# A mixture-of-experts stage with other load shapes, another gather and another order of its matmuls

## The chip, the cores and the metric

The kernel runs on one core of one Trainium2 chip. The metric is the device time of one execution in microseconds (us). The three runs of the kernel before took 984.13, 984.41 and 986.63 us, so the median is 984.41 us. The profile was taken of one execution by the hardware profiler.

A core has five engines with instruction streams of their own: TensorE (PE, whose weight loads are listed as PEld), VectorE (DVE), ScalarE (ACT), GpSimd (POOL) and SyncE (SP), which here issues the DMAs. They meet through semaphores. The matrix memory SBUF has 128 partitions; matmuls write to eight banks of PSUM, 512 fp32 words wide.

## The reference

One decoder layer on 512 tokens of width 1024. The part that matters here is the second of its three blocks, a mixture of 32 experts of which every token uses two:

```python
u = rms_norm(h, norm_ffn_g[l])
# every token: the best of 4 groups, in it the best 2 of 8 experts, with gates from two softmaxes
# every expert e, for the rows that chose it (fp32):
h_e = silu(x_e @ w_gate_e[e]) * (x_e @ w_up_e[e])     # (rows, 1024) @ (1024, 512), twice
y_e = h_e @ w_down_e[e]                               # (rows, 512) @ (512, 1024)
h = h + sum over the two choices of gate * y
```

Ahead of it stands a recurrent and pooling block (dense projections, about the first 370 us of the profile), behind it a gated per-layer embedding (`h + sigmoid(u @ w_ple_gate) * (p @ w_ple)`) and a last RMSNorm. The weights of the experts are 32 x 3 x 2 MB = 201 MB.

## The kernel before

Tokens are held as four tiles of 128 rows (`TT` = 4), the width as eight k-tiles of 128 (`KD`), an expert's hidden width of 512 as four (`KF`). `ring` is a ring of eight slots of 2 MB in SBUF; the three matrices of an expert (gate, up, down) each fill one slot. The SP stream loads matrix m + 8 into the slot of matrix m once PE has read that one (`wait_expert_read`), so at most eight matrices are loaded or in use, and SP's loads go out in the order in which PE reads them.

An expert takes up to `C` = 64 rows in one round. The number of rounds is read from a register (`rounds_i`); for these inputs one round runs. Inside it a loop runs four times over a body of eight experts (`UNROLL`), so PE, DVE, ACT, POOL and SP all branch back three times. For each expert:

- DVE makes `pick`, a 0/1 matrix [token, row] per token tile, by comparing `iota` with `place` (L975), and copies that expert's `info` (row number and gate) to `pinfo` (L1027).
- PE gathers the rows: `pick` is the stationary operand (64 columns), the normed tokens `u2` the moving one, in fp32, two halves of the width into the upper and lower 64 partitions of bank 0. ACT copies them to `xrow` (L731), PE transposes them (L1261), ACT copies the result to `xT` (L735). With `gather_info` PE also brings row number and gate into row order, and DVE's `take_info` copies them out (L1030, L1031).
- PE multiplies `xT` with gate and up (L1117, 128x256 moving, 32 matmuls; each fp32 matmul appears twice in the trace), again in two halves of partitions of bank 2.
- ACT takes the sigmoid (L746), DVE multiplies twice (L1048, L1050), PE transposes the hidden rows (L1294), DVE copies them to `hT` (L1052).
- PE multiplies `hT` with down (128x512 moving), DVE scales by the gate (L1058), and POOL scatters the 64 rows to `expert_rows` in HBM (L558). Four buffers `yrow` are in turn; `row_free` says that a scatter has landed.

On PE the order within an expert is: gate and up of e, gather for e + 1, transposes of hidden(e), info of e + 1, transposes of the rows of e + 1, down of e. Every line that goes through the helper `mm` shows as L1117, so in the trace the tiles and shapes tell the matmuls apart.

After the last expert SP waits for the last scatter and loads `expert_rows` back in eight pieces (L465); DVE adds them to the residual `h1` (L1070); POOL and DVE make the low parts of `w_ple_gate` (L339) from the high parts that ACT rounded (L755). Two-part operands exist there and in the dense blocks: a value is rounded to fp32r (`high`) and the rest kept as fp32r too (`low`); an fp32r matmul appears once in the trace.

## Time and profile before

| what | us |
|---|---|
| runs, lowest / median / highest | 984.13 / 984.41 / 986.63 |
| span of the profiled execution, first to last instruction (no time apart from its span is given for it) | 986.3 |
| first gate matmul of expert 0 to the end of the down product of expert 31 | 395.45 to 905.4 |
| PE busy over the span | 923.1 (94%) |
| DVE / ACT / POOL busy | 369.2 / 259.6 / 129.0 |
| bytes moved by DMA | 255.12 MB, of these 248.46 MB on SP's queue |
| mean granted TensorE clock | 0.967 of full |

A span's rows can be read on four levels. The page gives shares of the whole span; the timeline gives single instructions (start, duration, engine, line, operation, tiles, shapes, count; in brackets the idle time before and what ended it); windows give busy time and the granted clock of a stretch; the DMA view gives bytes and packets of each queue. TensorE's ends are modelled, so what one matmul costs in a row of matmuls is read from the distance between starts. The page says that the chain of waits that ended last is 78% PE, 13% DVE, and that DMA is busy for nine tenths and more in every slice from about 415 us to 890 us.

### The profile page before, as it was taken

How to read it: one execution, taken by the hardware profiler on the slowest of the kernel's cores; microseconds unless marked ns; L12 is line 12 of the kernel's file. 1: busy time of each engine (PE TensorE's matmuls, PEld its weight loads, DVE VectorE, ACT ScalarE, POOL GpSimd, SP SyncE). 2: the span in 40 equal slices, each digit the busy share in tenths (PEclk: the TensorE clock that was granted, in tenths of full speed). 3: DMA queues.
4: the chain of work that ended last, by engine and by line, in shares of the span. 5: the costliest groups of instructions: out<-in, count | busy, mean ns of one | idle time of the engine just before them, and what ended most of it. 6: DMA issues, size and time to landing. Idle time of an engine off the chain costs nothing.

```text
span 986.3 us, 13206 instructions
## 1 busy us (share of the span) xinstructions
PE 923.1 (94%) x5579; PEld 586.0 (59%) x5579; DVE 369.2 (37%) x580; ACT 259.6 (26%) x359; POOL 129.0 (13%) x85
## 2 busy tenths in 40 slices
PE   4999995999999996999998999989999899999796
PEld 3678773888888873545544554545455445554485
DVE  5699898464243424111111111111211121111764
ACT  6464445352132132111010101010101110112347
POOL 3328942000000000000000000000000000001320
PEclk8899997999999997999999999999999899999799
DMA  9122221122144749799999999999999999992702
GB/s 260 57 86 85 86 86 43 67 105 86 67 147 171 276 174 359 252 398 394 396 393 396 394 397 394 396 394 392 394 395 394 391 391 394 395 396 84 274 1 86
DMA packets 112898, 255.12 MB, mean 259 GB/s; under 512 B 8562, under 2 KB 9654, under 8 KB 112840
## 3 DMA queue, kind: packets, MB, share of 16 engines
q1 hardware_dynamic: 109848, 248.46, 67.7%
q0 software_dynamic: 2560, 4.20, 1.2%
q10 hardware_dynamic: 432, 1.57, 0.4%
q8 instruction: 49, 0.80, 0.3%
q14 instruction: 9, 0.07, 0.0%
HBM read 247.93 MB, written 10.49 MB: 262 GB/s over the span
## 4 chain that ended last, share of the span: by engine, by line
PE 78%; DVE 13%; ACT 3%; issue 2%; SPq 2%; DMA 2%; DVEq 0%; POOLq 0%; ACTq 0%
PE bank L1117 74%; DVE ring L873 2%; DVE ring L877 2%; PE bank L1261 2%; PE bank L1294 1%; DVE ring L885 1%; DVE ring L859 1%; DVE r L879 1%; DMA ring<-in_w_in_dram 1%; DVE r L1070 1%; PE bank L1131 1%; DVE ring L878 1%; SPq L395 1%; ACT ring_rounded L324 1%; DVE ring L875 1%
## 5 line engine op out<-in xcount | busy, mean ns | idle before, releaser
L1117 PE MATMUL bank<-ring_rounded,ring_rounded 128*128 128x512 f32 x704 | 248.0, 396 | 1.7 <-ACT ring L760 1.7
L1117 PE MATMUL bank<-ring,junk 128*64 128x256 f32 x2048 | 232.7, 386 | 9.7 <-issue 8.9
L1117 PE MATMUL bank<-r_rounded,ring_rounded 128*128 128x512 f32 x704 | 232.9, 402 | 1.4 <-DVE ring_rounded L817 1.3
L1117 PEld LDWEIGHTS bank<-ring,junk 128*64 128x64 f32 x2048 | 150.0, 140 | 100.7 <-issue 33.6
L1117 PE MATMUL bank<-r 128*64 128x512 f32 (+2 forms) x1064 | 147.8, 405 | 11.4 <-ACT ring L633 10.1
L1117 PEld LDWEIGHTS bank<-r_rounded,ring_rounded 128*128 128x128 f32 x704 | 134.2, 191 | 33.6 <-issue 2.9
L1117 PEld LDWEIGHTS bank<-ring_rounded,ring_rounded 128*128 128x128 f32 x704 | 134.4, 191 | 32.7 <-issue 2.9
L1117 PE MATMUL bank<-ring,r 128*64 128x512 f32 (+1 forms) x544 | 132.8, 600 | 3.8 <-DVE ring L859 3.8
L1117 PEld LDWEIGHTS bank<-r 128*64 128x64 f32 (+1 forms) x1064 | 58.4, 139 | 82.7 <-issue 76.7
L558 POOL DMA_INDIRECT expert_rows<-r,row_i x32 | 31.3, 978 | 553.4 <-DVE r L1058 553.4
L746 ACT ACTIVATE r<-bank 128x256 f32<-128x256 f32 x32 | 12.3, 383 | 324.8 <-PE bank L1117 324.8
L1048 DVE TENSOR_TENSOR r<-r,bank 128x256 f32<-128x256 f32 x32 | 13.5, 421 | 213.7 <-ACT r L746 213.7
L1117 PEld LDWEIGHTS bank<-ring,r 128*64 128x64 f32 (+1 forms) x544 | 39.8, 139 | 69.2 <-issue 64.0
L1058 DVE TENSOR_SCALAR r<-bank,gate_c 128x512 f32<-128x512 f32 x32 | 24.0, 751 | 124.4 <-PE bank L1117 124.4
L324 ACT ACTIVATE ring_rounded<-ring 128x2048 fp32r<-128x2048 f32 x28 | 53.5, 1912 | 41.5 <-DMA ring<-in_w_in_dram 18.9
L329 POOL TENSOR_TENSOR ring_rounded<-ring,ring_rounded 128x2048 fp32r<-128x2048 f32 x11 | 53.6, 4877 | 74.5 <-ACT ring_rounded L324 74.3
L1117 PE MATMUL bank<-ring_rounded,r_rounded 128*128 128x512 f32 x128 | 50.8, 397 | 0.0
L731 ACT ACTIVATE r<-bank 128x512 f32<-128x512 f32 x33 | 19.7, 597 | 105.1 <-PE bank L1117 105.1
L329 DVE TENSOR_TENSOR ring_rounded<-ring,ring_rounded 128x2048 fp32r<-128x2048 f32 x17 | 39.0, 2294 | 15.0 <-ACT ring_rounded L324 14.8
L1052 DVE COPY r<-bank 128x256 f32<-128x256 f32 x32 | 13.6, 424 | 80.0 <-PE bank L1294 80.0
L1131 PE MATMUL bank<-ident,r 128*128 128x128 f32 x96 | 16.0, 325 | 17.2 <-DVE r L809 17.2
L1117 PEld LDWEIGHTS bank<-ring_rounded,r_rounded 128*128 128x128 f32 x128 | 24.6, 192 | 5.2
(172 smaller groups left out, 622.4 us busy)
## 6 DMA issues: line engine op xcount, KB each, us to landing
ring<-in_w_gate_e_dram SPq DMA_DIRECT2D x32, 2048.0 KB, 19.6
ring<-in_w_up_e_dram SPq DMA_DIRECT2D x32, 2048.0 KB, 18.4
ring<-in_w_down_e_dram SPq DMA_DIRECT2D x32, 2048.0 KB, 19.1
ring<-in_w_in_dram SPq DMA_DIRECT2D x18, 1024.0 KB, 7.1
r<-in_x_dram SPq DMA_DIRECT2D x8, 512.0 KB, 8.0
ring<-in_w_up_a_dram SPq DMA_DIRECT2D x4, 1024.0 KB, 6.1
ring<-in_w_out_dram SPq DMA_DIRECT2D x4, 1024.0 KB, 6.2
ring<-in_w_ple_gate_dram SPq DMA_DIRECT2D x2, 2048.0 KB, 21.0
```

What stands on the lines that cost most here:

```text
L324: nc.scalar.activation(high_half(n, h), whole_half(n, h), ACT.Copy).then_inc(high_ready, 1)
L329: api.tensor_tensor(low_half(n, h), whole_half(n, h), high_half(n, h), ALU.subtract).then_inc(low_ready[low_engine[n, h]], 1)
L558: nc.gpsimd.indirect_dma_start(out=y_halves, out_offset=bass.IndirectOffsetOnAxis(ap=row_i[:, m:m + 1], axis=0), in_=yrow[:, m % 4, :], in ...
L731: nc.scalar.activation(xrow, bank[0][:, :], ACT.Copy).then_inc(xrow_ready, 1)
L873: after(v.reciprocal(q, q))
L877: after(v.tensor_tensor(t, t, q, ALU.mult))
L1048: v.tensor_tensor(hid, sig, bank[2][:, 0:FE // 2], ALU.mult).then_inc(gated, 1)
L1052: v.tensor_copy(hT.rearrange("p (h j) c -> p j h c", h=2), bank[3][:, 0:FE // 2].rearrange("p (j h c) -> p j h c", j=2, h=2)).then_inc(hT_ ...
L1058: v.tensor_scalar(yrow[:, m % 4, :], bank[5][:, :], gate_c[:, m:m + 1], None, ALU.mult).then_inc(y_stored, 1)
L1117: return nc.tensor.matmul(*a, **k)
L1131: ins = nc.tensor.transpose(bank[banks[q % 4]][:, k * P:(k + 1) * P], src[:, i % TT, (4 * h + k) * P:(4 * h + k + 1) * P], ident[:, :])
L1261: ins = nc.tensor.transpose(bank[4][:, j * P:(j + 1) * P], xrow[:, j * P:(j + 1) * P], ident[:, :])
```

## The change

1. The unit of work is a pair of experts. `pick` holds both (128 columns), and one gather per half of the width brings 128 rows. The moving operand is `u2` split in two fp32r parts, `u2_high` (rounded by ACT) and `u2_low` (three tiles by DVE, the last by POOL). Each half takes eight fp32r matmuls, one half beside each expert of the pair before. `xrow` (now in `gain`) and `xT` hold both experts.
2. Gate and up are read from HBM as `(p k) n` where it was `(k p) n`: eight adjacent rows of 512 words go to one partition, one run of 16 KB where there were eight of 2 KB. Down has runs of 8 KB (two adjacent rows of 1024 words, twice per partition) where there were four of 4 KB. For the matmuls to match, the norm writes `u2` in the order of these k-tiles, the router weights are loaded by the same rule, and DVE writes the hidden rows with a stride.
3. The down product of expert e - 1 stands behind gate and up of e; gate and up alternate between banks 2 and 3. The load order follows (`loads`).
4. No inner loop: 32 experts stand in one row of code, inside the loop over rounds alone. At the end of each round the rows of the next round's first pair are gathered (`first_pair`), for the last round too.
5. `pinfo` and its copies are gone; `info` and `place` lose their 33rd entry. The gain of the next norm is loaded after the stage, since `xrow` lies in its place. Both halves of `w_ple_gate` are issued ahead of the loads of `expert_rows`.

The diff, cut to its core:

```diff
+    loads = [(0, 0), (1, 0)]
+    for e in range(1, NE):
+        loads += [(0, e), (1, e), (2, e - 1)]
+    loads += [(2, NE - 1)]
...
+        xT = junk[:, :].rearrange("p (k e c) -> p k e c", k=KD, e=2)
+        xrow = gain[:, :]
+        u2_low = r2_r[:, :].rearrange("p (i d) -> p i d", i=TT)
+        u2_high = r3_r[:, :].rearrange("p (i d) -> p i d", i=TT)
+        pick = sb("pick", [P, TT, 2, C], F32R)
...
+        def split_u2(eng, api, i):
+
+            eng.wait_ge(u2_high_ready, i + 1)
+            eng.wait_ge(ut_psum, 2 * (TT + i) + 2)
+            api.tensor_tensor(u2_low[:, i, :], u2[:, i, :], u2_high[:, i, :], ALU.subtract).then_inc(u2_low_ready, 1)
...
-            def load_expert(m, e):
-
-                n, k, w = m, (KD, KD, KF)[m % 3], (w_gate_e, w_up_e, w_down_e)[m % 3]
-                src = w[0, e].rearrange("(k p) n -> p k n", p=P) if isinstance(e, int) else \
-                    w[0, bass.ds(e, 1)].rearrange("o (k p) n -> p (o k) n", p=P)
-                sp.dma_start(wslot(n, k), src).then_inc(slot_full[n % SLOTS], 16)
-
+            def load_expert(n):
+
+                which, e = loads[n % (3 * NE)]
+                dst = ring[:, n % SLOTS, :]
+                if which < 2:
+
+                    src = (w_gate_e, w_up_e)[which][0, e].rearrange("(p k) n -> p (k n)", p=P)
+                else:
+
+                    src = w_down_e[0, e].rearrange("(h p j) n -> p h (j n)", h=2, p=P)
+                    dst = dst.rearrange("p (h w) -> p h w", h=2)
+                sp.dma_start(dst, src).then_inc(slot_full[n % SLOTS], 16)
...
+                for n in range(SLOTS, 3 * NE):
+                    wait_expert_read(n)
+                    load_expert(n)
...
+                with sp.Else():
+
+                    wait_expert_read(3 * NE)
+                    sp.dma_start(wple, w_ple[0].rearrange("(k p) n -> p k n", p=P)).then_inc(slot_full[s0], 16)
+                    sp.dma_start(p_rows, p[0, 0].rearrange("(i p) n -> p i n", p=P)).then_inc(slot_full[s0], 16)
+                    for h in range(2):
+                        wait_expert_read(3 * NE + T_PG + h)
+                        sp.dma_start(wslot(T_PG + h, KD), wg[:, :, h * HALF:(h + 1) * HALF]).then_inc(slot_full[T_PG + h], 16)
...
-            sp.dma_start(wslot(T_PG + 1, KD), wg[:, :, HALF:D]).then_inc(slot_full[T_PG + 1], 16)
...
+            def u2_round(i):
+
+                act.wait_ge(norm_done, TT + i + 1)
+                nc.scalar.activation(u2_high[:, i, :], u2[:, i, :], ACT.Copy).then_inc(u2_high_ready, 1)
...
+            def first_pair(at):
+                copy_rows(at, 0)
+                copy_rows(at, 1)
+                copy_xT(at, 0)
+                copy_xT(at, 1)
...
+                n0 = act.snap(r * NE)
+                for e in range(NE):
+                    act.wait_ge(gate_up_psum, n0 + (e + 1))
+                    if e >= 1:
+                        act.wait_ge(hidden_ready, n0 + e)
+                    nc.scalar.activation(sig[:, :], bank[2 + e % 2][:, 0:FE // 2], ACT.Sigmoid).then_inc(sig_ready, 1)
+                    if e < NE - 2:
+                        at = n0 + (2 * (e // 2 + 1))
+                        copy_rows(at, e % 2)
+                        if e % 2 == 1:
+                            copy_xT(at, 0)
+                            copy_xT(at, 1)
+                first_pair(n0 + NE)
+            act.dma_start(gain[:, :], norm_ple_g[0].partition_broadcast(P)).then_inc(gain_in, 16)
...
-                        normalise(c, h1[:, c - TT, :], u2[:, c - TT, :])
+                        normalise(c, by_tile(h1[:, c - TT, :]), u2[:, c - TT, :].rearrange("p (k q) -> p q k", k=KD), by_tile)
...
+                    dve.wait_ge(sig_ready, n0 + (e + 1))
+                    v.tensor_tensor(sig[:, :], sig[:, :], gate_up[:, 0:FE // 2], ALU.mult).then_inc(gated, 1)
+                    dve.wait_ge(gated, n0 + (e + 1))
+                    v.tensor_tensor(hid[:, :].rearrange("p (j q) -> p q j", j=2), sig[:, :].rearrange("p (q j) -> p q j", j=2),
+                                    gate_up[:, FE // 2:FE].rearrange("p (q j) -> p q j", j=2), ALU.mult).then_inc(hidden_ready, 1)
+                    if e % 2 == 0 and e < NE - 2:
+                        take_info(e + 2, n0 + (e + 3))
+                    if e >= 1:
+                        scale_y(n0, e - 1)
+                    copy_hT(n0, e)
+                    if e % 2 == 1 and e < NE - 2:
+                        take_info(e + 2, n0 + (e + 3))
+                        if e < NE - 3:
+                            make_pick(e // 2 + 2)
+                scale_y(n0, NE - 1)
                 v.tensor_scalar(place[:, :, :], place[:, :, :], -float(C), None, ALU.add).then_inc(next_round, 1)
                 dve.wait_ge(next_round, r + 1)
+                make_pick(0)
+                take_info(0, n0 + (NE + 1))
+                take_info(1, n0 + (NE + 2))
+                make_pick(1)
...
-            def gather(b):
-
+            def gather(h):
+
+                for i in range(TT):
+                    for part in (u2_high, u2_low):
+                        ins = mm(bank[6 + h][:, :], pick[:, i, :, :].rearrange("p e c -> p (e c)"),
+                                 part[:, i, h * HALF:(h + 1) * HALF], start=(i == 0 and part is u2_high),
+                                 stop=(i == TT - 1 and part is u2_low))
+                ins.then_inc(xrow_psum, 1)
...
+            def first_pair(n0, picks):
+                pe.wait_ge(pick_ready, picks)
+                gather(0)
+                gather(1)
+                transpose_x(n0, 0)
+                transpose_x(n0, 1)
+                pe.wait_ge(info_made, 2)
+                gather_info(0)
+                pe.wait_ge(info_ready, n0 * 2 + 2)
+                gather_info(1)
...
+                for e in range(NE):
+                    gate_and_up(n0, e)
+                    if e < NE - 2:
+                        pe.wait_ge(pick_ready, r * PAIRS + (e // 2 + 2))
+                        gather(e % 2)
+                        if e % 2 == 0:
+                            pe.wait_ge(info_ready, n0 * 2 + 2 * (e + 2))
+                            gather_info(e + 2)
+                    if e >= 1:
+                        down(n0, e - 1)
+                    if e % 2 == 1 and e < NE - 2:
+                        transpose_x(n0 + (e + 1), 0)
+                        transpose_x(n0 + (e + 1), 1)
+                    transpose_hidden(n0, e)
+                    if e % 2 == 1 and e < NE - 2:
+                        pe.wait_ge(info_ready, n0 * 2 + 2 * (e + 2))
+                        gather_info(e + 2)
+                down(n0, NE - 1)
+                pe.wait_ge(info_ready, n0 * 2 + 2 * NE)
+                first_pair(n0 + NE, r * PAIRS + (PAIRS + 1))```

How the instructions move, at three places. First PE inside the stage, before: one expert and the start of the next (`r` holds pick and rows or hidden rows, `junk` is `xT`).

```order
L1117 MATMUL bank<-ring,junk 64x256 x32
L1290 REGISTER_ALU
L1117 MATMUL bank<-r 64x512 x8
L1294 MATMUL bank<-ident,r 128x128 x2
L1117 MATMUL bank<-r 64x2 x8
L1298 REGISTER_ALU
L1261 MATMUL bank<-ident,r 128x128 x4
L1117 MATMUL bank<-ring,r 64x512 x8
L1117 MATMUL bank<-ring,junk 64x256 x32
```

PE in the changed kernel, from the last two of the eight gather matmuls of an odd expert to gate and up of the next (`gain` is `xrow`, `r_rounded` the two parts of `u2`).

```order
L1158 MATMUL bank<-r_rounded_59,pick 128x512
L1158 MATMUL bank<-r_rounded_58,pick 128x512
L1158 MATMUL bank<-ring,hT 64x512 x8
L1302 REGISTER_ALU
L1304 MATMUL bank<-ident,gain 128x128 x4
L1302 REGISTER_ALU
L1304 MATMUL bank<-ident,gain 128x128 x4
L1337 MATMUL bank<-ident,hid 128x128 x2
L1371 REGISTER_ALU
L1158 MATMUL bank<-info,pick 64x2 x8
L1158 MATMUL bank<-ring,junk 64x256 x32
```

Down has moved ahead of the transposes of the hidden rows and belongs to the expert before; the row transposes of two experts stand together once per pair.

Second, the end of the stage on DVE, before: the last expert's scaling, the step of `place`, and the copy for the embedding.

```order
L1058 TENSOR_SCALAR r<-bank,gate_c 128x512
L1040 REGISTER_ALU
L1040 COMPARE_AND_BRANCH
L1061 ISA
L1062 TENSOR_SCALAR place<-place 128x132
L1063 REGISTER_ALU
L1039 REGISTER_ALU
L1039 COMPARE_AND_BRANCH
L1066 COPY ring<-bank 128x512
```

And in the changed kernel, from the same scaling (L1067) to the end of the round.

```order
L1067 TENSOR_SCALAR r<-bank,gate_c 128x512
L1099 TENSOR_SCALAR place<-place 128x128
L1100 REGISTER_ALU
L1012 TENSOR_TENSOR pick<-iota,place 128x512
L1060 REGISTER_ALU
L1061 TENSOR_SCALAR row_i<-bank,row_base 128x1
L1062 COPY gate_c<-bank 128x1
L1060 REGISTER_ALU
L1061 TENSOR_SCALAR row_i<-bank,row_base 128x1
L1062 COPY gate_c<-bank 128x1
L1012 TENSOR_TENSOR pick<-iota,place 128x512
```

Six instructions for the next round's first pair now stand between the last scaling and the copy that serves the embedding.

Third, SP behind the last expert's loads, before.

```order
L457 DMA ring<-in_w_ple_dram 128x2x1024
L458 DMA ring<-in_p_dram 128x4x256
L460 DMA ring<-in_w_ple_gate_dram 128x8x512
L454 UNCONDITIONAL_BRANCH
L437 REGISTER_ALU
L437 COMPARE_AND_BRANCH
L436 REGISTER_ALU
L436 COMPARE_AND_BRANCH
L462 ISA
L465 DMA ring<-expert_rows 128x1024 x8
L467 DMA ring<-in_w_ple_gate_dram 128x8x512
```

SP in the changed kernel.

```order
L469 DMA ring<-in_w_ple_dram 128x2x1024
L470 DMA ring<-in_p_dram 128x4x256
L457 REGISTER_ALU
L473 DMA ring<-in_w_ple_gate_dram 128x8x512 x2
L466 UNCONDITIONAL_BRANCH
L451 REGISTER_ALU
L451 COMPARE_AND_BRANCH
L475 ISA
L478 DMA ring<-expert_rows 128x1024 x8
```

The second half of `w_ple_gate` has moved ahead of the eight loads of `expert_rows`.

## Rows read from the trace of the kernel before

**Rows 1.** The page: the span

```profile
span 986.3 us, 13206 instructions
```

**Rows 2.** Timeline of PE and ACT, 600 to 634 us: start, us, engine line operation

```profile
600.92 7.08 PE L1117 MATMUL bank<-ring,junk 128*64 128x256 f32 x64
...
607.83 3.60 PE L1117 MATMUL bank<-r 128*64 128x512 f32 x16
...
611.36 0.44 PE L1294 MATMUL bank<-ident,r 128*128 128x128 f32 x2
611.48 0.60 ACT L731 ACTIVATE r<-bank 128x512 f32<-128x512 f32 x1 [3.05 <-PE bank L1117]
...
611.73 0.63 PE L1117 MATMUL bank<-r 128*64 128x2 f32 x16
...
612.30 0.66 PE L1261 MATMUL bank<-ident,r 128*128 128x128 f32 x4
...
612.88 3.65 PE L1117 MATMUL bank<-ring,r 128*64 128x512 f32 x16
...
616.37 7.08 PE L1117 MATMUL bank<-ring,junk 128*64 128x256 f32 x64
```

**Rows 3.** Waits, 450 to 880 us: us in total, times, longest

```profile
PE bank L1117 <- issue: 8.9, 3, 3.0
```

**Rows 4.** Timeline of PE where the loop branches back

```profile
522.16 8.63 PE L1117 MATMUL bank<-ring,junk 128*64 128x256 f32 x64 [2.94 <-issue]
```

**Rows 5.** Windows there: busy of PE, PEld, DVE, ACT, POOL, clock, DMA, GB/s

```profile
522.00:525.00 3.00, 2.84 (x14) 1.72 (x16) 0.00 (x0) 0.00 (x0) 0.00 (x0) 0.50 1.04 393
```

**Rows 6.** Timeline of SP's queue: the last expert load

```profile
866.93 5.35 SPq L423 DMA_DIRECT2D ring<-in_w_down_e_dram  x1
```

**Rows 7.** DMA by queue, 490 to 880 us: packets, MB, share of 16 engines

```profile
q1 hardware_dynamic: 62317, 150.10, 101.5%
...
q8 instruction: 27, 0.44, 0.5%
```

**Rows 8.** DMA by queue, 379 to 382 us: a down load alone

```profile
q1 hardware_dynamic: 319, 1.24, 103.7%
```

**Rows 9.** DMA by queue, 95 to 110 us: dense weights, runs of 2 KB

```profile
q1 hardware_dynamic: 1056, 2.10, 38.9%
```

**Rows 10.** Timeline of PE, dense block: fp32r matmuls, 128 columns, 512 moving

```profile
332.56 1.30 PE L1117 MATMUL bank<-ring_rounded,ring_rounded 128*128 128x512 f32 x5
333.69 0.39 PE L1117 MATMUL bank<-ring_rounded,r_rounded 128*128 128x512 f32 x1
```

**Rows 11.** Timeline of DVE and PE at the start of the stage

```profile
370.54 1.28 DVE L809 SCALAR_TENSOR_TENSOR r<-r,rstd,gain 128x1024 f32<-128x1024 f32 x1
...
386.76 0.43 DVE L975 TENSOR_TENSOR r<-iota,place 128x256 f32<-128x256 f32 x1
...
387.24 6.47 PE L1117 MATMUL bank<-r 128*64 128x512 f32 x32 [1.23 <-DVE r L975]
...
395.45 6.91 PE L1117 MATMUL bank<-ring,junk 128*64 128x256 f32 x62 [0.80 <-ACT junk L735]
```

**Rows 12.** Timeline behind the last down product, 905 to 915 us

```profile
905.38 1.09 PE L1316 MATMUL bank<-ident,ring 128*128 128x128 f32 x8
905.49 0.75 DVE L1058 TENSOR_SCALAR r<-bank,gate_c 128x512 f32<-128x512 f32 x1 [3.89 <-PE bank L1117]
...
907.00 3.61 ACT L755 ACTIVATE ring_rounded<-ring 128x4096 fp32r<-128x4096 f32 x1
...
910.99 4.76 SPq L465 DMA_DIRECT2D ring<-expert_rows  x8
...
911.37 8.83 POOL L339 TENSOR_TENSOR ring_rounded<-ring,ring_rounded 128x4096 fp32r<-128x4096 f32 x1 [3.36 <-DMA expert_rows<-r,row_i]
...
914.59 9.10 DVE L1070 TENSOR_TENSOR r<-r,ring 128x1024 f32<-128x1024 f32 x3 [7.31 <-DMA ring<-expert_rows]
```

**Rows 13.** The instructions of L1070: count, duration ns min/median/max

```profile
L1070 DVE TENSOR_TENSOR r<-r,ring x8: 1216/1222/6701, 914.6 to 940.5; 128x1024 f32<-128x1024 f32 x8
```

More of the change, by code:

```diff
@@ L33 @@
 C = 64
-UNROLL = 8
 BIG = 1e30
@@ new lines, in _ @@
+                n0 = pe.snap(r * NE)
+                for e in range(NE):
+                    gate_and_up(n0, e)
[14 more added lines that the diff above has]
+                        gather_info(e + 2)
```

293 lines of the change are left out of this document (123 added, 170 removed).

## The prediction

> **What bounds the kernel now.** I went from the page to the waits, then to PE's timeline, SP's queue and the DMA view. The profiled execution spans 986.3 us [rows 1]; I add up against it and take off 1.9 us at the end, its distance from the median of the runs, 984.41.
>
> In the expert stage PE never idles for data: in 430 us its only idle time is 8.9 us in three pieces, released by nothing that the profile shows [rows 3]. So PE's own work is the bound. Timeline starts give it: gate and up 600.92 to 607.83 = 6.91 us, gather 3.53, hidden transposes 0.37, info 0.57, row transposes 0.58, down 3.49; together 15.45 us per expert, and the next begins at 616.37 [rows 2]. 32 x 15.45 = 494.4 us. The stage takes 509.9 us (395.45 [rows 11] to T, the end of the last down product, 905.38 [rows 12]). The other 15.5 us are the three branches back of the inner loop: each has 2.94 us without work and then a gate and up of 8.63 instead of 7.08 us [rows 4, 2] at a granted clock of 0.50, the lower level of 1.2 GHz, after that idle time [rows 5].
>
> The reader should also see that DMA has no reserve. SP's queue moves 150.10 MB in 390 us at 101.5% of 16 engines [rows 7]: one load of 2.097 MB per 5.45 us, while PE wants one per 15.45 / 3 = 5.15 us. Only the eight slots that are full at the start hide this, and issuing the last load takes SP 5.35 us, so the queue is backed up [rows 6]. For 88 loads behind the first eight DMA needs 88 x 5.45 = 480 us of PE's 510. A faster PE alone would soon run into DMA. The two halves of this change, less PE work and longer runs, therefore have to be priced together.
>
> **PE's work.** Gather: a pair now costs 16 fp32r matmuls of 128 columns by 512. Five such, started at 332.56, and the next at 333.69 give 0.226 us each [rows 10], so 3.62 us per pair where two gathers cost 7.06. The rest is moved, not removed: row transposes 1.16 and info 1.14 per pair, hidden transposes, gate, up and down as before. Sum: 32 x (6.91 + 3.49 + 0.37) + 15 x (3.62 + 1.16 + 1.14) = 344.6 + 88.8 = 433.4 us, 13.7 per expert. The loop borders' 15.5 us go as well; that straight code fetches without such a stop is what the eight experts between two borders show.
>
> Do new waits eat this? Before, ACT's and DVE's steps between up and the hidden transposes fitted into the 3.53 us of gather, since the transposes follow it without a gap at 611.36, and the copy to `hT` into the 1.15 us ahead of down [rows 2]. Now the first have 1.8 us of gather and 3.5 of down, the second a whole gate and up. The rows' transposes wait for an ACT copy of 0.60 us [rows 2] that lies beside 3.5 us of down. xT is single, but the copy of its first half (0.6 us) lies beside 0.6 us of further transposes, 0.4 of hidden ones and 0.6 of info. The strided hidden write can double DVE's 0.4 us and stays covered. I add 0.8 us once, for the last expert, whose down has no cover. If a cover failed at every pair, it would cost 16 x 0.5 = 8 us.
>
> **DMA.** Runs of 16 and 8 KB don't occur on SP's queue now, so I bound. A 2 KB packet costs 38.9% x 16 x 15 us / 1024 (32 of the 1056 are tiny) = 91 ns [rows 9]; a 4 KB packet 103.7% x 16 x 3 us / 303 (16 tiny) = 164 ns [rows 8]. That is 18 ns fixed and 36.5 per KB. An engine's share of an expert is 128 packets of 2 KB and 32 of 4 KB, 16.9 us; with 16 of 602 ns and 16 of 310 ns it would be 14.6 us, so a load takes 5.45 x 14.6 / 16.9 = 4.71 us. At the 4 KB cost for everything it is 5.45 x 15.7 / 16.9 = 5.08. Below nothing: the only 16 KB packets in the trace are 27 of the instruction queue at 0.5% x 16 x 390 / 27 = 1.16 us [rows 7], another target; at that cost a load would take over 9 us. I take 5.0 us, near the measured 4 KB row, because the scatters share the engines.
>
> The row says that 4 KB packets move at 25 bytes per ns and engine against 22.5 at 2 KB [rows 8, 9]. The Trainium skill (DMA: Bandwidth & Descriptors, "Why small descriptors are slow") gives a fixed overhead of about three bus cycles per packet, 3 on top of 64 at 2 KB; by it alone the mean overhead would fall from 3.9% to 0.8%, a load to 5.45 x 1.008 / 1.039 = 5.29 us, and the sum would end near 960 us. The trace has the larger fixed part (18 of 91 ns), and I go by it.
>
> **The start.** Gate of expert 0 begins 8.2 us after the first gather [rows 11]. Now both halves (the same 16 passes) come first, then copy 0.6, transposes 0.58, info 0.57, a copy of 0.4, info 0.57 and hops: 9.4. POOL's split of the last tile of `u2` is a quarter of 8.83 us, 2.2 [rows 12]; where a POOL subtraction ran, a DVE addition took 6.70 instead of 1.22 us [rows 12, 13], so up to 1.5 us of the router chain can be held. Start +2.7 us (0 to +5): 398.15. The strided norm may double its 1.28 us [rows 11] but lies ahead of a PE that is still busy with the projection or the router, and the other splits fall into DVE's and ACT's waits: nothing.
>
> **The stage's end T.** By DMA: 398.15 + 3.46 (gate of 0 read) + 2.2 (issue to data: 910.99 to 914.59 [rows 12] less 1.4 for its half megabyte) + 88 x 5.0 + 3.5 (last down) = 847.3. By PE: 398.15 + 433.4 + 0.8 = 832.3. DMA ends last: 905.4 becomes 847.3, a gain of 58.1. What is late next is the weight: PE will wait about 15 us in all for slots, in the second half of the stage.
>
> **The tail.** Before, the first add that counts ends at T + 15.9: it starts at 914.59, is held 6.70 us while POOL subtracts from 911.37 to 920.20, and POOL had ACT's rounding of 3.61 us from 907.00 [rows 12, 13]. Now the next round's first pair stands ahead: scaling 0.75, place and pick about 1.1, gathers 3.6, copy and transposes 1.2, info, copy, info 1.5, so the transposes for the embedding begin at T + 8.4 instead of T. Then 1.1, a copy 0.6, rounding 3.6: POOL subtracts from T + 13.8 to T + 22.6 and the add ends at T + 23.8. That is +7.8. If POOL does not meet the adds, DMA still delays them: 5.8 MB of embedding weights stand in SP's queue ahead of `expert_rows`, 15 us at the present rate from T - 3.5, so the rows land 4 to 5 us later than at 914.59. So +4.5 to +7.8, and I take 7.8. The second half of `w_ple_gate` arrives earlier, which nothing waits for.
>
> **Sum.** 986.3 - 58.1 + 7.8 = 936.0 on the profile, 934 as a median.
>
> **Rivals.**
> - *PE stays the bound.* Long runs reach 4.8 us a load or better (4.71 by the packet fit). T = 832.3, 921 on the profile, 919 as a median, 916 with the short tail. For: the fit. Against: nothing on SP's queue runs above 25 bytes per ns.
> - *Longer runs are cut or give little.* At 5.1 to 5.3 us a load, 5.2: T = 864.9, 953.6 less 1.9 = 952.
> - *The rate stays.* The change then doesn't do what it says: 5.45 us, T = 886.9, 975.6 less 1.9 = 974. For: 101.5% busy already, so a limit behind the engines could bind. Against: the 4 KB packets do better.
> - *Long runs are slower: a slower kernel.* The engines now read addresses 64 KB apart, each fills one partition for 16 KB, and if that clashes in HBM or SBUF, each load waits in the ring. From 5.57 us a load (T = 897.5, plus the tail) the kernel is slower than before, only 2.2% above today's 5.45; at 6.0 us T = 935.3 and the time 1022. For: the costly 16 KB packets [rows 7], and how little reserve there is. Against: they go elsewhere, and 4 KB runs are already better than 2 KB ones.
>
> The Trainium skill (the same page, "Latency and other measured facts") speaks for the last: row pitches of large powers of two slow a copy, 207 GB/s at 512 KiB and 103 at 4 MiB against a full 214. No run here shows such a pitch yet. The pitch here is 16 KB; by its smallest entry a load of 5.0 would be 5.17 us and the time 949.
>
> **How the numbers follow.** Forecast (4.85 to 5.1 us a load) 0.58, PE bound 0.17, cut runs 0.12, rate unchanged 0.07, slower 0.05, and 0.01 for a gain eaten altogether. A measurement of this kernel tells about 0.3% (3 us) from no change. Faster by more: 0.94; within: 0.01; slower: 0.05. The likeliest case's own range is 918 to 946 us. The range of 8 in 10 runs from 914 (PE bound, short tail) to 960 (cut runs at 5.3 us), which leaves the last rivals out.
>
> **What would show it.** Packets of 16 and 8 KB, a fifth as many per expert (512 where there were 2560); 415 to 420 GB/s in the stage's second half, with PE waiting there for DMA and not before about 600 us; 13.7 us per expert before that; no idle PE of 3 us inside the stage; gate of expert 0 at about 398; the POOL subtraction some 14 us behind the last down. I am wrong if PE waits for DMA from the first experts on (rate), if PE's own period exceeds 13.9 us with weights there (a cover failed, or fp32r and fp32 side by side cost something), or if the granted clock falls in the small waits.

## The result and the profile after

| kernel | median of runs, us | lowest to highest | runs |
|---|---|---|---|
| before | 985.45 | 984.13 to 986.63 | 4 |
| changed | 947.17 | 943.69 to 948.42 | 4 |

The ratio is 0.9603 with a 95% interval of 0.9584 to 0.9622: 38 us less. The forecast was 934 us, its range 914 to 960. The profiled execution of the changed kernel took 943.69 us with a span of 941.9; it is the fastest of the four, the other three have spans of 945.1 to 946.7.

The page of the changed kernel (span; queue row; the chain that ended last, by engine):

```profile
span 941.9 us, 12475 instructions
...
q1 hardware_dynamic: 44312, 248.46, 65.2%
...
PE 61%; DMA 18%; DVE 14%; ACT 3%; SPq 2%; issue 1%; DVEq 0%; ACTq 0%; POOLq 0%
```

The same 248.46 MB come in 44312 packets; before's page has 109848 on this queue. DMA now has 18% of the chain, where it had 2%, and PE waits for weights, most of all for those of up. The waits between 380 and 880 us (us in total, times, longest) answer to [rows 3]:

```profile
PE bank L1158 <- DMA ring<-in_w_up_e_dram: 11.0, 11, 2.6
...
PE bank L1158 <- DMA ring<-in_w_down_e_dram: 4.2, 3, 1.6
...
PE bank L1158 <- DMA ring<-in_w_gate_e_dram: 1.1, 2, 0.9
```

The three pieces of issue time are gone; 16.3 us of waiting for weights have come, the first of it ahead of the matmul at 690.30 us. PE's timeline of a pair (start, us), which answers to [rows 2]:

```profile
588.15 7.11 PE L1158 MATMUL bank<-ring,junk 128*64 128x256 f32 x64
595.19 2.11 PE L1158 MATMUL bank<-r_rounded,pick 128*128 128x512 f32 x8
597.23 0.63 PE L1158 MATMUL bank<-info,pick 128*64 128x2 f32 x16
597.71 3.63 PE L1158 MATMUL bank<-ring,hT 128*64 128x512 f32 x16
601.28 0.44 PE L1337 MATMUL bank<-ident,hid 128*128 128x128 f32 x2
601.65 7.13 PE L1158 MATMUL bank<-ring,junk 128*64 128x256 f32 x64
608.70 2.11 PE L1158 MATMUL bank<-r_rounded,pick 128*128 128x512 f32 x8
610.74 3.65 PE L1158 MATMUL bank<-ring,hT 128*64 128x512 f32 x16
614.33 1.09 PE L1304 MATMUL bank<-ident,gain 128*128 128x128 f32 x8
615.25 0.38 PE L1337 MATMUL bank<-ident,hid 128*128 128x128 f32 x2
615.57 0.63 PE L1158 MATMUL bank<-info,pick 128*64 128x2 f32 x16
616.05 2.14 PE L1158 MATMUL bank<-ring,junk 128*64 128x256 f32 x18
```

From 588.15 to 616.05 are 27.90 us for a pair, 13.95 per expert, with no idle time: nothing waits for ACT or DVE. The gathers take 2.04 us each by their starts.

The DMA view by queue, 490 to 840 us, which answers to [rows 7]:

```profile
q1 hardware_dynamic: 12938, 145.13, 98.2%
```

145.13 MB in 350 us are 414.7 GB/s, one load of 2.097 MB per 5.06 us. The stage's start and what stands behind the last down product (timelines of several engines), which answer to [rows 11, 12]:

```profile
387.00 5.71 PE L1158 MATMUL bank<-r_rounded,pick 128*128 128x512 f32 x16 [1.59 <-DVE pick L1012]
...
396.29 3.89 PE L1158 MATMUL bank<-ring,junk 128*64 128x256 f32 x34 [0.65 <-issue]
...
852.81 3.65 PE L1158 MATMUL bank<-ring,hT 128*64 128x512 f32 x16 [0.98 <-DMA ring<-in_w_down_e_dram]
...
864.98 1.69 PE L1383 MATMUL bank<-ident,ring 128*128 128x128 f32 x8
...
870.46 12.14 DVE L1111 TENSOR_TENSOR r<-r,ring 128x1024 f32<-128x1024 f32 x3 [3.07 <-DMA ring<-expert_rows]
...
870.89 9.49 POOL L343 TENSOR_TENSOR ring_rounded<-ring,ring_rounded 128x4096 fp32r<-128x4096 f32 x1 [11.86 <-ACT ring_rounded L785]
...
887.48 0.73 PE L1158 MATMUL bank<-ring_rounded,ring_rounded 128*128 128x512 f32 x2 [1.72 <-ACT ring L790]
```

The last down ends at T = 852.81 + 3.65 = 856.5 (905.4 before). The gating product starts at T + 31.0; before it started at 929.39, T + 24.0. One of the three adds takes 9.74 us:

```profile
L1111 DVE TENSOR_TENSOR r<-r,ring x8: 1212/1222/9741, 870.5 to 896.9; 128x1024 f32<-128x1024 f32 x8
```

### The profile page after: what moved, and what is told of

It reads as the page before. It is cut to its first block, busy times and chain, and to the rows that moved or that the text cites. A ratio compares the mean times of both kernels' runs of the same rounds, so it can differ in the third digit from the quotient of the medians.

```text
span 941.9 us, 12475 instructions
## 1 busy us (share of the span) xinstructions
PE 871.0 (92%) x5343; PEld 587.6 (62%) x5343; DVE 380.6 (40%) x535; ACT 258.8 (27%) x362; POOL 132.0 (14%) x86
## 3 DMA queue, kind: packets, MB, share of 16 engines
q1 hardware_dynamic: 44312, 248.46, 65.2%
## 4 chain that ended last, share of the span: by engine, by line
PE 61%; DMA 18%; DVE 14%; ACT 3%; SPq 2%; issue 1%; DVEq 0%; ACTq 0%; POOLq 0%
PE bank L1158 59%; DMA ring<-in_w_up_e_dram 11%; DMA ring<-in_w_down_e_dram 4%; DVE ring L906 2%; DVE ring L910 2%; DVE ring L918 1%; DVE ring L892 1%; DVE r L1111 1%; PE bank L1304 1%; DVE r L912 1%; DMA ring<-in_w_in_dram 1%; DMA ring<-expert_rows 1%; PE bank L1172 1%; PE bank L1337 1%; DVE ring L911 1%
## 5 line engine op out<-in xcount | busy, mean ns | idle before, releaser
L1158 PE MATMUL bank<-ring_rounded,ring_rounded 128*128 128x512 f32 x704 | 245.4, 392 | 1.7 <-ACT ring L790 1.7
L1158 PE MATMUL bank<-ring,junk 128*64 128x256 f32 x2048 | 230.2, 381 | 12.8 <-DMA ring<-in_w_up_e_dram 11.0
L1158 PE MATMUL bank<-r_rounded,ring_rounded 128*128 128x512 f32 x704 | 231.4, 400 | 2.1 <-DVE ring_rounded L850 1.3
L1158 PEld LDWEIGHTS bank<-ring,junk 128*64 128x64 f32 x2048 | 143.3, 137 | 88.7 <-DMA ring<-in_w_up_e_dram 16.0
L1158 PEld LDWEIGHTS bank<-r_rounded,ring_rounded 128*128 128x128 f32 x704 | 133.6, 190 | 34.3 <-issue 2.9
L1158 PEld LDWEIGHTS bank<-ring_rounded,ring_rounded 128*128 128x128 f32 x704 | 132.5, 189 | 32.1 <-issue 2.8
L1158 PE MATMUL bank<-ring,hT 128*64 128x512 f32 x512 | 116.6, 597 | 4.2 <-DMA ring<-in_w_down_e_dram 4.2
L1085 DVE TENSOR_TENSOR sig<-sig,bank 128x256 f32<-128x256 f32 x32 | 13.5, 421 | 224.2 <-ACT sig L770 224.2
L770 ACT ACTIVATE sig<-bank 128x256 f32<-128x256 f32 x32 | 12.3, 384 | 300.9 <-PE bank L1158 300.9
L1158 PE MATMUL bank<-r_rounded,pick 128*128 128x512 f32 x272 | 72.9, 412 | 3.3 <-DVE pick L1012 3.3
L1158 PEld LDWEIGHTS bank<-ring,hT 128*64 128x64 f32 x512 | 34.0, 137 | 65.5 <-issue 59.4
L1067 DVE TENSOR_SCALAR r<-bank,gate_c 128x512 f32<-128x512 f32 x32 | 24.0, 751 | 118.2 <-PE bank L1158 118.2
L1158 PEld LDWEIGHTS bank<-r_rounded,pick 128*128 128x128 f32 x272 | 49.9, 193 | 25.3 <-issue 13.2
L1158 PE MATMUL bank<-ring_rounded,r_rounded 128*128 128x512 f32 x128 | 49.9, 389 | 0.0
L747 ACT ACTIVATE gain<-bank 128x512 f32<-128x512 f32 x34 | 20.3, 597 | 71.2 <-PE bank L1158 71.2
L751 ACT ACTIVATE junk<-bank 128x512 f32<-128x512 f32 x34 | 18.7, 594 | 54.1 <-PE bank L1304 54.1
L1172 PE MATMUL bank<-ident,r 128*128 128x128 f32 x96 | 16.1, 325 | 13.3 <-DVE r L842 13.3
L597 ACT ACTIVATE junk<-r 128x1024 f32<-128x1024 f32 x16 | 16.9, 1059 | 37.4 <-DVE r L958 29.4
```

What stands on the lines that cost most here:

```text
L597: after(nc.scalar.activation(junk[:, :], src, ACT.Square, accum_out=ssq[:, q:q + 1]))
L747: nc.scalar.activation(xrow[:, h * HALF:(h + 1) * HALF], bank[6 + h][:, :], ACT.Copy).then_inc(xrow_ready, 1)
L751: nc.scalar.activation(xT[:, 4 * h:4 * h + 4, :, :].rearrange("p k e c -> p k (e c)"), bank[6 + h][:, :].rearrange("p (k n) -> p k n", k=4 ...
L1067: v.tensor_scalar(yrow[:, e % 4, :], bank[5][:, :], gate_c[:, e:e + 1], None, ALU.mult).then_inc(y_stored, 1)
L1085: v.tensor_tensor(sig[:, :], sig[:, :], gate_up[:, 0:FE // 2], ALU.mult).then_inc(gated, 1)
L1158: return nc.tensor.matmul(*a, **k)
```

## Experiments

The theory: PE's shorter work and the end of the loop's stops only move the limit from PE to SP's queue; the longer runs lower that limit; each alone is worth little. Kernels named "before with" carry one part of the change, kernels named "changed with" lack one or have an edit of their own. The ratios are to the kernel before, measured beside them.

**1. Before with no inner loop.**

```diff
-UNROLL = 8
+UNROLL = 32
```

> Part 4 alone: the kernel before with a body of 32 experts instead of 8, so no branch back inside a round. Theory (PE's own work bounds the kernel before, and a border costs 2.94 us without work and about 2.2 us at the lower clock): 3 x 5.2 = 15.5 us less, 970 us, no idle PE of 3 us in the stage, T (end of the last down product) near 890 on the trace. Rival (DMA was about to bind, and its 5.45 us a load ends the stage at about 893 to 895 whatever PE does): 972 to 975. Rival (straight code of this length stops for its instructions all the same): 984.

Measured: 976.22 us (976.09 to 977.11), ratio 0.991 (0.9893 to 0.9926). PE at the place of [rows 4], and its waits from 400 to 895 us:

```profile
520.54 7.08 PE L1117 MATMUL bank<-ring,junk 128*64 128x256 f32 x64
```

```profile
PE bank L1117 <- DMA ring<-in_w_up_e_dram: 1.7, 3, 0.6
```

The stops and the slow matmuls behind them are gone. T goes from 905.4 to 893.8, though expert 0's gate began 1.5 us later in this execution (396.95 for 395.45): the stage itself shrinks by 13.1 us, to 496.8, for the 15.5 I had priced, and 1.7 us of the rest stand as waits for weights. The time lies 6 us above what the theory said; the spans of the profiled executions differ by 11.8 us, the medians by 9.3. The rival's T of 893 to 895 was met too: PE alone would have been through at 396.95 + 494.4 = 891.4, so the two limits lie within 2.4 us of each other. The loop's stops were worth 9 to 12 us, with DMA already close.

**2. Before with long runs only** (gate, up and down loads, the norm's order, router rows and hidden write go with them).

```diff
-                src = w[0, e].rearrange("(k p) n -> p k n", p=P) if isinstance(e, int) else \
...
+                if m % 3 < 2:
+                    src = src.rearrange("(p k) n -> p (k n)", p=P)
+                else:
+                    src = src.rearrange("(h p j) n -> p h (j n)", h=2, p=P)
```

> Part 2 alone: the kernel before with runs of 16 and 8 KB (and the order of u2, router weights and hidden rows that goes with them). Theory (DMA is hidden in the kernel before): no change, 984 to 987 us; SP's issues stay at about 0.4 us through the whole stage instead of growing to 5 us, and SP's queue is busy under 101%. Rival (DMA traffic slows PE or the rows come too late somewhere): 975 or less.

Measured: 984.82 us (983.09 to 989.67), ratio 0.9999 (0.9982 to 1.0017). Waits of PE from 450 to 880 us:

```profile
PE bank L1126 <- issue: 8.7, 3, 3.0
```

DMA by queue, 490 to 820 us:

```profile
q1 hardware_dynamic: 11360, 128.19, 95.4%
```

The runs are long, the queue now has room (95.4% busy, 5.40 us a load, which is only what PE asks for), and the time does not move. Nobody waited for the loads.

**3. Changed, with the short runs of before.**

```diff
-                    src = (w_gate_e, w_up_e)[which][0, e].rearrange("(p k) n -> p (k n)", p=P)
+                    src = (w_gate_e, w_up_e)[which][0, e].rearrange("(k p) n -> p k n", p=P)
...
-                    src = w_down_e[0, e].rearrange("(h p j) n -> p h (j n)", h=2, p=P)
+                    src = w_down_e[0, e].rearrange("(k p) n -> p k n", p=P)
```

> The changed kernel without part 2: runs of 2 and 4 KB as before, u2, router weights and hidden rows in the old order. Theory (weight loads end the stage): 88 x 5.45 us instead of 88 x 5.06 us, so 34 us later than the changed kernel, about 980 us; PE waits for DMA from about expert 5 on. Rival (PE's work and start-up waits carry most of the stage, the loads only the end): under 965 us.

The order of `u2`, the router rows and the hidden write go back with them. Measured: 981.13 us (977.76 to 983.25), ratio 0.9956 (0.9937 to 0.9974). PE's waits from 380 to 888 us:

```profile
PE bank L1158 <- DMA ring<-in_w_up_e_dram: 34.0, 17, 3.2
...
PE bank L1158 <- DMA ring<-in_w_gate_e_dram: 5.5, 10, 1.3
...
PE bank L1158 <- DMA ring<-in_w_down_e_dram: 1.0, 1, 1.0
```

DMA by queue, 490 to 820 us:

```profile
q1 hardware_dynamic: 52721, 127.11, 101.6%
```

127.11 MB in 330 us are 5.44 us a load, the rate of before, with 40.5 us of waits. The time is what the theory said (980). Runs 2 and 3 together are the point of the case: long runs alone 0%, everything else alone 0.4%, both 4.0%.

The 0.4% needs one remark: it is less than run 1's 0.9%, which carries one part of the same change, and the intervals do not overlap. T is 888.5 here (884.82 + 3.65), 5.3 us ahead of run 1's, but behind it come 87.6 us for run 1's 80.7. So the shorter PE work did bring T forward, and the longer tail ate it.

**4. Changed, with half the bytes.** From the ninth load on each load brings half of its matrix, so the output is not the reference's; PE, DVE and ACT do all their work.

```diff
+                if n >= SLOTS:
+                    src, dst = (src[:, 0], dst[:, 0]) if which == 2 else (src[:, 0:SLOT // 2], dst[:, 0:SLOT // 2])
```

> The changed kernel with half the bytes of every expert load behind the first eight (the other half of a slot keeps what it had, so the output is not the reference's). It shows PE's own pace in this order of instructions. Theory: 27.9 us a pair throughout, T near 837, about 20 us less than the changed kernel, near 926 us, the granted clock 1.0 throughout the stage. Rival (PE's waits for other engines or the clock take over in the second half too): over 935 us.

Measured: 925.74 us (923.02 to 929.23), ratio 0.9385 (0.9347 to 0.9424). DMA by queue, 490 to 820 us:

```profile
q1 hardware_dynamic: 10839, 74.43, 66.6%
```

The one wait of PE between 450 and 840 us that remains, and the last down product:

```profile
PE bank L1160 <- DVE hT L1073: 0.9, 1, 0.9
```

```profile
837.18 3.65 PE L1160 MATMUL bank<-ring,hT 128*64 128x512 f32 x16 [0.91 <-DVE hT L1073]
```

T = 840.8 is PE's own pace; with all bytes it is 856.5. The loads therefore cost about 16 us of T, the sum of PE's waits above (16.3). The medians lie further apart, 20.6 us from the unedited kernel beside it (946.37, run 7): the tail is 1.1 to 2.4 us shorter here than in the two traces of the changed kernel, and what is left is within their spread.

**5. Changed, with down in its own expert again.**

```diff
-                    if e >= 1:
-                        down(n0, e - 1)
...
+                    down(n0, e)
```

> The changed kernel without part 3: down of expert e stands behind its own hidden transposes, loads in the order gate, up, down of each expert, one scaling earlier on DVE. Theory (loads end the stage): within 2 us of the changed kernel, 945 to 949 us, and on the trace a PE period of 27.9 us a pair in the first half as with part 3. Rival (without down ahead of them the hidden transposes wait for ACT and DVE): 0.5 to 1 us more per expert in the first half, 14.5 us per expert, and still little in the time.

Measured: 947.11 us (943.84 to 952.11), ratio 0.9601 (0.9577 to 0.9625), the same as the changed kernel's 0.9603. The profiled execution is the slowest of its four. PE's waits from 450 to 870 us:

```profile
PE bank L1153 <- DVE hT L1068: 9.1, 15, 0.6
PE bank L1153 <- DMA ring<-in_w_up_e_dram: 5.1, 5, 1.5
PE bank L1332 <- DVE hid L1084: 3.1, 2, 1.6
```

A wait of 0.6 us per pair comes for `hT`, so a pair takes 28.50 us (600.66 to 629.16) where the theory said 27.9; the rival's wait is real, but 0.3 us per expert and not 0.5 to 1. The waits for weights shrink from 16.3 us to 5.3. What PE loses early it would have waited for later. The place of the down product is worth nothing while the loads set the end.

**6. Changed, with both halves' gathers in one place.**

```diff
-                        gather(e % 2)
...
+                            gather(0)
+                            gather(1)
```

> The changed kernel with the gather products of both experts of a pair, 16 fp32r matmuls, in one place behind the even expert's gate and up instead of 8 behind each expert's. In the changed kernel one group of 8 takes 2.04 us from the first start to the next engine step, of which 8 by 0.226 would be 1.81. Theory (the rest, 0.23 us, is paid once per group, when TensorE goes over from fp32 to fp32r): the group of 16 takes 3.85 us, a pair of experts 27.67 us instead of 27.90 while nothing waits for loads, and the whole time does not move (within 1.5 us), since the loads set the end. Rival (every fp32r matmul costs 0.255 us beside this kernel's work): the group of 16 takes 4.08 us and the pair stays at 27.90.

Measured: 945.33 us, one run. PE's timeline of a pair:

```profile
586.78 7.11 PE L1160 MATMUL bank<-ring,junk 128*64 128x256 f32 x64
593.82 3.92 PE L1160 MATMUL bank<-r_rounded,pick 128*128 128x512 f32 x16
597.67 0.63 PE L1160 MATMUL bank<-info,pick 128*64 128x2 f32 x16
...
602.09 7.13 PE L1160 MATMUL bank<-ring,junk 128*64 128x256 f32 x64
609.05 3.60 PE L1160 MATMUL bank<-ring,hT 128*64 128x512 f32 x16
612.58 1.09 PE L1306 MATMUL bank<-ident,gain 128*128 128x128 f32 x8
...
614.31 7.11 PE L1160 MATMUL bank<-ring,junk 128*64 128x256 f32 x64
```

16 matmuls take 3.85 us (16 x 0.226 = 3.62, and 0.23 once), the pair 27.53 us instead of 27.90. So the step from fp32 to fp32r costs about 0.23 us, by this difference. The pair's further 0.14 us lie where the second gather stood: gate and up take 6.96 us there for 7.05 (601.65 to 608.70), and the down behind them 3.53 for 3.59, near the 6.91 and 3.49 of the kernel before, where no fp32r matmul stands beside them. One stretch of fp32r matmuls among fp32 ones costs 0.37 us in all. The whole time stays, as the loads set it: PE waits 16.1 us for weights and 5.8 us more for which the profile names nothing, ahead of down products from 666 us on; together that is 5.6 us more than in the changed kernel.

**7. The tail: four kernels.** Changed again, unedited, as a measure of its own spread:

> The changed kernel once more, beside the next three on one chip: 944 to 949 us, T at about 856 to 860 on the trace.

Measured: 946.37 us (943.96 to 948.29), ratio 0.9596 (0.9563 to 0.9628).

Without the first pair of a round that never comes:

```diff
-                first_pair(n0 + NE)
+                with act.If(n0 < final):
+                    first_pair(n0 + NE)
```

> The changed kernel without the gather of a next round's first pair behind the last round (PE, ACT and DVE branch past it, and past the step of place). Theory (the tail grew because this work pushes POOL's subtraction onto DVE's additions): transposes for the embedding at T instead of T + 8.5, POOL subtracts from about T + 5.5 to T + 14.5, the additions then meet no POOL and the second ends near T + 17 instead of T + 25; 6 to 8 us less, about 940 us. Rival (the tail waits for expert_rows behind the embedding weights in SP's queue, landing at T + 14 either way): at most 2 us less.

Measured: 944.29 us (943.64 to 945.67), ratio 0.9577 (0.9549 to 0.9604). The theory of 6 to 8 us failed and the rival's "at most 2 us" came: ACT's rounding now waits 3.90 us for the first half of `w_ple_gate`, so POOL begins at T + 9.7 and not at T + 5.5, and the adds meet it again.

With the second half of `w_ple_gate` behind the loads of `expert_rows`:

```diff
-                    for h in range(2):
+                    for h in range(1):
...
+            sp.dma_start(wslot(T_PG + 1, KD), wg[:, :, HALF:D]).then_inc(slot_full[T_PG + 1], 16)
```

> The changed kernel with the second half of w_ple_gate behind the loads of expert_rows again. First theory (POOL's subtraction holds the additions): the rows land 5 us earlier, the first two additions then fit in ahead of POOL, but the norm behind them is held to POOL's end at T + 24, so 2 to 3 us less, about 945 us. Rival (landing sets the tail): 5 us less, about 942 us.

Measured: 943.6 us (941.03 to 946.8), ratio 0.9579 (0.9541 to 0.9617). As the theory said, two adds now stand ahead of POOL, the third takes 8.74 us, and the norm starts at T + 24.0. Both edits at once:

> The changed kernel with the first pair of the round that never comes left out, and the second half of the embedding gate's weights asked for behind the expert-output rows; POOL keeps its subtraction. Each edit alone gave 944.3 and 943.6 us for 946.4 to 947.2. Theory (POOL's subtraction and the three adds share one stretch whatever comes first): the rows land 2 to 4 us earlier than in either alone, POOL's subtraction starts near T+10, and the norm starts when subtraction and one add are through, near T+21 to T+22: 941 to 943 us. Rival (the two edits are independent savings of 2.1 and 2.8 us): 941.5 to 942.3. Rival (both save the same wait): 943.5 to 944.5.

Measured: 944.8 us (944.52 to 944.96), ratio 0.9585 (0.9569 to 0.9601), longer than the theory and both rivals said (941 to 944.5). Each alone gave 2 to 3 us by the medians, both together no more, and all intervals overlap that of the unedited kernel, so at most some 2 us are there. DVE and POOL in the kernel with both edits:

```profile
868.45 8.82 POOL L343 TENSOR_TENSOR ring_rounded<-ring,ring_rounded 128x4096 fp32r<-128x4096 f32 x1 [6.89 <-ACT ring_rounded L788]
868.86 11.89 DVE L1116 TENSOR_TENSOR r<-r,ring 128x1024 f32<-128x1024 f32 x3 [7.72 <-DMA ring<-expert_rows]
```

Whatever is made earlier, the adds still meet POOL's subtraction and end with it. The last kernel takes both edits and moves that subtraction to DVE, behind the first two adds:

```diff
-            gate_low(pool, nc.gpsimd, 0)
...
+            gate_low(dve, v, 0)
```

> The changed kernel with three edits behind the last expert: the first pair of a round that never comes is left out, the second half of the embedding gate's weights is asked for behind the expert-output rows again, and the one subtraction of the gate that stood on POOL (121 or so columns wide over all tokens, 9.49 us there) is done by DVE behind the first add of expert rows. Theory (POOL's subtraction is what holds DVE's second add, 9.75 us for 1.22): with no POOL work beside them the adds take 1.2 to 1.3 us each, the first add starts when the rows land, 14.1 us or so behind the last down product (870.6 against T 856.5), three adds cost 3.7 us and the subtraction 1 to 2 us more on DVE, so the first norm starts near T+20 instead of T+26.8, and the time is 5 to 6 us below the kernel with only the first two edits, 936 to 939 us, a ratio of 0.951 to 0.954. Rival A (the adds are held by transfers into SBUF, not by POOL): the second add stays at 8 us or more, and the time is 941 to 944. Rival B (the landing of the rows sets it and the subtraction on DVE eats the gain): adds of 1.2 us but the norm no earlier than T+25, 941 to 944 too; the two rivals differ in the add's duration.

(The subtraction is 128x4096, as the rows show; the width in the text above was wrong.) Measured: 940.29 us (939.39 to 943.17), ratio 0.9549 (0.9529 to 0.957): the best version, some 6 us below the changed kernel, 45 below the kernel before, and 4.5 below the kernel with the first two edits. The subtraction's move was not run without them. The instructions of the adds (count, ns min/median/max), then DVE's and PE's timeline:

```profile
L1115 DVE TENSOR_TENSOR r<-r,ring x8: 1216/1222/1226, 867.0 to 891.9; 128x1024 f32<-128x1024 f32 x8
```

```profile
869.58 4.42 DVE L343 TENSOR_TENSOR ring_rounded<-ring,ring_rounded 128x4096 fp32r<-128x4096 f32 x1
...
880.40 1.22 PE L1163 MATMUL bank<-ring_rounded,ring_rounded 128*128 128x512 f32 x2 [1.67 <-ACT ring L792]
```

With nothing on POOL no add takes more than 1.23 us: rival A of that run, transfers that hold the adds, is out. The Trainium skill (SBUF — State Buffer, "SBUF: two separate sides") says that a GpSimd instruction that reads SBUF and a VectorE instruction with two SBUF inputs take one port pair in turn, for a whole instruction each, and that DMA does not contend with engines there; the rows agree: the held add of the changed kernel ends at 881.5, 1.1 us behind POOL's 870.89 + 9.49 = 880.4. The gating product starts at T + 23.2 (T = 857.2) instead of T + 31.0, but the tail shrinks only from 85.4 to 80.4 us. The rest went to the clock: from the first gating matmul to the end it takes 57.2 us where the changed kernel took 54.4. Windows of the kernel with all three edits and of the changed one (busy of PE, PEld, DVE, ACT, POOL, then the clock):

```profile
880.00:887.00 7.00, 6.60 (x21) 5.33 (x21) 3.91 (x5) 1.92 (x5) 0.00 (x0) 0.53 0.36 135
```

```profile
887.00:897.00 10.00, 9.52 (x46) 7.67 (x47) 7.98 (x11) 6.10 (x10) 0.00 (x0) 1.00 0.01 2
```

After 3.35 and 1.67 us of idle time PE begins the gating at the lower level of 1.2 GHz (its pair of matmuls takes 1.22 us), where in the changed kernel PE had been idle for 0.91 and 1.72 us and the pair takes 0.73. That full clock is not a property of the changed kernel. In the trace of its second measurement above, PE was idle for 2.24 and 1.72 us ahead of the gating, and there the pair takes 1.22 us as well:

```profile
888.46 1.22 PE L1158 MATMUL bank<-ring_rounded,ring_rounded 128*128 128x512 f32 x2 [1.72 <-ACT ring L790]
```

That is T + 31.0 again (T = 857.4), but from there to the end it needs 55.7 us, and its tail is 86.8 us. Against it the three edits give 6.4 us, near the 6.1 of the medians. My estimate of 936 to 939 us left that out, and DVE needs 4.42 us for the subtraction where I had put 1 to 2.

## Why the prediction was right, and what was mis-sized

The direction, the two limits and their order held: PE first, the loads from the middle of the stage on, and a longer tail. On one basis, the profiled spans, 936.0 was forecast and 941.9 came: T is 9.2 us later than forecast, the tail 3.3 us shorter than forecast. So two errors of opposite sign met, and that the sum lies within 6 us of the forecast is in part luck. The remaining 7.2 us of the 13.1 between 934.1 and 947.17 is how profile and median stand to each other: I took off 1.9 us, since before's profiled span lay that much above its median, but the changed kernel's profiled execution is the fastest of its four, and its span lies 5.3 us below the median.

- **Start.** Forecast +2.7, measured +0.84 (396.29 for 395.45). The chain from the first gather to the first gate takes 9.29 us, as worked out (9.4), and the first gather is 0.24 us earlier; the 1.5 us for an addition held by POOL's split did not come. The second trace of the changed kernel has 398.16, but 1.5 us of that lag is there at 370 us already, ahead of the router. From one execution to the next the start moves by 1.9 us, more than the 0.84 measured.
- **PE.** The step "Five such ... give 0.226 us each, so 3.62 us per pair" holds inside the row of matmuls, but a pair pays 2 x 2.04 = 4.08. The forecast pair was 27.46, the measured one 27.90: gate and up take 7.04 and 7.05 us for 6.91, down 3.57 and 3.59 for 3.49, the gathers 0.46 us more, and the row transposes, info and hidden transposes together 0.47 less than the terms of before. Run 6 shows that the gathers and what stands beside them lose 0.37 us by each change to fp32r and back. The prediction's own sign, a period above 13.9 us with weights there since "fp32r and fp32 side by side cost something", came with 13.95. "PE stays the bound" would have been T = 840.8 and a time of 926 (run 4), not 832.3 and 919. No cover failed: the hidden write took 0.62 us for 0.42 and stayed hidden. Nor did the granted clock fall in the waits: it is 1.00 from 400 to 690 us and from 690 to 853 us.
- **DMA rate.** Forecast 5.0 us a load, measured 5.06, 5.3 us over 88 loads. The packet fit was right, and its scaling was not. Without the tiny ones (16 per load) 11831 packets of 16 and 8 KB filled 98.2% of 16 engines for 350 us, 465 ns on average; the fit gives (602 + 310) / 2 = 456. An engine's expert is then 32 x 0.465 = 14.9 us, and 14.9 / 3 / 0.982 = 5.06. The 4.71 came from scaling 14.6 / 3 = 4.87 down by the 3% that the short packets' times add up to more than the span; with long ones they don't, and why is not shown. That the value at the 4 KB cost, 5.08, lies so near is chance: at that cost the mean would be 492 ns. The Trainium skill's three cycles per packet (DMA: Bandwidth & Descriptors, "Why small descriptors are slow") gave 5.29; against 5.44 with short runs and 5.06 with long ones the measured gain is larger than that rule's. The Trainium skill (the same page, "Latency and other measured facts") has entries on row pitches from 512 KiB on; 5.17 by the smallest of them is not borne out by 5.06 either. That queue 8's 16 KB packets cost 1.16 us each said nothing of SP's.
- **T by DMA.** This is the step that failed in size. `398.15 + 3.46 + 2.2 + 88 x 5.0 + 3.5` supposes that the 88th load lands when its bytes have passed. SP asked for the ninth load at 400.00, so data began near 402.2 (1.6 us earlier than that), and at 5.06 a load the last down would have started at 402.2 + 445.3 = 847.5; it started at 852.81. The DMA view of the changed kernel by queue, from 400 to 840 us and from 840 to 853 us:

```profile
q1 hardware_dynamic: 16103, 181.43, 98.0%
```

```profile
q1 hardware_dynamic: 1347, 5.06, 97.2%
```

Up to 853 us the queue moved 186.49 MB, and 88 loads are 184.55 MB. So 1.94 MB of later loads, the embedding weights with their packets under 8 KB, had passed before the last down was complete. The 16 engines are not level at the end, and a load is complete with the last of them: 1.94 MB at 414.7 GB/s are 4.7 us. The packets show it too, from 844 to 846 us and from 851 to 852 us:

```profile
DMA packets 164, 0.82 MB, mean 410 GB/s; under 512 B 9, under 2 KB 66, under 8 KB 76
```

```profile
DMA packets 192, 0.36 MB, mean 365 GB/s; under 512 B 9, under 2 KB 95, under 8 KB 188
```

Expert weights come in packets of 8 KB and more. By 844 us some engines are in the later loads (67 packets between 512 B and 8 KB), while others still move the last down at 851 us (4 packets of 8 KB). What sets them apart I did not test.
- **Waits.** About 15 us forecast, not before 600 us; 16.3 us came, from 690 us on.
- **Tail.** The embedding's transposes begin at T + 8.5 (forecast 8.4), POOL at T + 14.4 (13.8), the held add ends at T + 25.0 (23.8), the second add and not the first. The gating starts 7.0 us later behind T than before, and the tail is 4.5 us longer, not 7.8: from its first matmul to the end it needs 54.4 us for 56.9, since it starts at the full clock, where before's gating began at 929.39 like run 7's, with 1.22 us for the first two matmuls. That was chance: the second trace of the same kernel begins the gating at the lower level, and there the tail is 5.9 us longer than before's. Most of what the tail can give back came with run 7's subtraction (944.8 to 940.29 us), measured on top of the two other edits.

What is still open: what the gather alone would bring on the kernel before, which no run has; why the engines stand apart at the end of the loads; why long packets fill the engines to 98% and short ones to more than 100; and the changed kernel's spread of 5 us from run to run, which is as wide as what the single edits of run 7 could bring. Its two traces show parts of that spread ahead of the stage (1.5 us) and in the clock of the gating (1.3 us).

## What to carry to other kernels

When two resources are both near their limit (here PE at 15.45 us per expert and the queue at 3 x 5.45), price the relief of either alone and of both: the long runs alone were worth 0%, all the rest alone 0.4% (the loop's part alone 0.9%), together 4%. An engine made faster pays only until the next limit, so test edits that shorten it with the bytes halved before polishing them. And behind a stage's end, keep GpSimd's two-input work away from VectorE's adds of two SBUF operands, and look at the clock that the next product starts with, in more than one trace.

## What the runs showed of the hardware

- SP's queue moved 414.7 GB/s with 16 and 8 KB runs (385.2 with 2 and 4 KB ones) from HBM for 350 us, 425 GB/s over all queues. The Trainium skill (DMA: Bandwidth & Descriptors, "Bandwidth") has 425 GB/s for one large load, and this agrees; its limit of about 358 GB/s per core, given for both cores of a stack at work, did not bind with one.
- A packet of SP's queue cost 465 ns on average with runs of 16 and 8 KB in equal number, where the fit from the 2 and 4 KB packets of the kernel before (91 and 164 ns) gives 456.
- The last of a long row of loads landed about 4.7 us behind its share of the bytes, since some engines run ahead into the next loads.
- A change from fp32 to fp32r matmuls cost TensorE about 0.23 us (16 matmuls in 3.85 us, 8 in 2.04), and the change there and back 0.37 us.
- A VectorE add with two SBUF operands took 9.74 us for 1.22 beside a GpSimd subtraction of 9.49 us, and no more than 1.23 us once that was gone.
- From the first gating matmul to the end of the kernel it took 54.4 us in the trace whose first two matmuls took 0.73 us (full clock), and 55.7 us in the second trace of the same kernel, 56.9 in that of the kernel before and 57.2 in run 7's last, where they took 1.22 (the lower level).
